# Block products accumulated in PSUM banks, and a third crossed pair in the MLP's second matrix

## What is computed

```python
def sq_relu_mlp(y, w_up, w_down):
    u = y @ w_up
    return jnp.square(jax.nn.relu(u)) @ w_down

for i in range(DEPTH):
    y = rmsnorm(h, norm_gains[i, 0])
    ...
    h = h + y
    h = h + sq_relu_mlp(rmsnorm(h, norm_gains[i, 1]), mlp_w_up[i], mlp_w_down[i])
```

## Time and profile before

| what | value |
|---|---|
| time of the kernel, median of 3 runs | 1192.2 us (1191.93 to 1194.11) |
| profiled execution, first to last instruction | 1190.5 us |
| PE busy | 1177.8 us, 99% of the span, 8809 matmuls |
| DVE busy | 1012.5 us, 85% |
| ACT busy | 696.4 us, 58% |
| POOL busy | 114.4 us, 10% |
| mean granted TensorE clock | 0.997 |
| HBM traffic | 110 GB/s |

### The profile page before, as it was taken

The page is one execution under the profiler, slowest core; times in us unless marked ns, Lnnn a source line. Parts: engine busy times, 40 slices in busy tenths (PEclk is TensorE's granted clock), DMA queues, the critical chain, the costliest instruction groups (busy, mean ns, idle before and its releaser), DMA issues.

```text
span 1190.5 us, 22996 instructions
## 1 busy us (share of the span) xinstructions
PE 1177.8 (99%) x8809; PEld 1126.1 (95%) x8809; DVE 1012.5 (85%) x1623; ACT 696.4 (58%) x1201; POOL 114.4 (10%) x171
## 2 busy tenths in 40 slices
PE   9999999999999999999999999999999999999998
PEld 8999999999999999999999999987899988989988
DVE  6889888888889989998568988887898998999973
ACT  6777877745534544535357887876545355445453
POOL 3221110100110110101010000000001001001000
PEclk9999999999999999999999999999999999999999
DMA  7343342433463563673231212223336535546532
GB/s 179 95 113 85 89 109 77 146 110 106 109 143 106 116 136 107 148 208 111 57 104 54 68 57 78 80 69 119 100 132 126 132 118 113 124 124 143 162 106 72
DMA packets 152376, 131.89 MB, mean 111 GB/s; under 512 B 23208, under 2 KB 143072, under 8 KB 152288
## 3 DMA queue, kind: packets, MB, share of 16 engines
q1 hardware_dynamic: 141600, 104.93, 29.9%
q0 software_dynamic: 10560, 25.66, 10.9%
q10 hardware_dynamic: 128, 0.09, 0.0%
HBM read 111.43 MB, written 19.24 MB: 110 GB/s over the span
## 4 chain that ended last, share of the span: by engine, by line
PE 64%; issue 22%; DVE 8%; ACT 3%; DMA 1%; POOL 1%; SPq 0%; DVEq 0%; POOLq 0%; ACTq 0%
PE ps L2335 24%; PE ps L2027 18%; PE ps L2262 15%; PE ps L2553 2%; PE ps L2082 1%; DVE lo L1611 1%; ACT hi L741 1%; PE ps L2100 1%; DVE u L1662 1%; DVE tbuf L1662 1%; DVE lof L1604 1%; DMA h_sum<-abuf 1%; DVE tbuf L1667 1%; DVE lo L1618 1%; ACT ah L1029 1%
## 5 line engine op out<-in xcount | busy, mean ns | idle before, releaser
L741 ACT ACTIVATE hi<-lof 128x1024 fp32r<-128x1024 f32 x80 | 82.8, 1052 | 136.6 <-DVE lof L1604 136.6
L2027 PE MATMUL ps<-yh,wh 128*128 128x264 f32 (+1 forms) x704 | 160.5, 302 | 0.0
L2027 PE MATMUL ps<-yh,wl 128*128 128x264 f32 (+1 forms) x704 | 155.3, 295 | 0.0
L2027 PE MATMUL ps<-yl,wh 128*128 128x264 f32 (+1 forms) x704 | 155.3, 294 | 0.0
L2335 PE MATMUL ps<-th,hi 128*128 128x264 f32 (+1 forms) x448 | 127.0, 283 | 0.5 <-DVE tbuf L1662 0.5
L2335 PE MATMUL ps<-tl,hi 128*128 128x264 f32 (+1 forms) x448 | 126.4, 282 | 0.0
L2335 PE MATMUL ps<-th,lo 128*128 128x264 f32 (+1 forms) x448 | 126.3, 282 | 0.0
L2262 PE MATMUL ps<-ah,hi 128*128 128x264 f32 (+1 forms) x448 | 116.3, 318 | 0.3
L1611 DVE TENSOR_TENSOR lo<-lof,hi 128x1024 fp32r<-128x1024 f32 x80 | 97.1, 1222 | 22.1 <-ACT hi L741 20.5
L2262 PE MATMUL ps<-al,hi 128*128 128x264 f32 (+1 forms) x448 | 115.6, 316 | 0.0
L2262 PE MATMUL ps<-ah,lo 128*128 128x264 f32 (+1 forms) x448 | 115.4, 316 | 0.0
(11 more groups left out here) (332 smaller groups left out, 3370.6 us busy)
## 6 DMA issues: line engine op xcount, KB each, us to landing
raw<-in_mlp_w_up_dram SPq DMA_DIRECT2D x32, 1024.0 KB, 5.6
raw<-in_mlp_w_down_dram SPq DMA_DIRECT2D x32, 1024.0 KB, 5.0
raw<-in_diff_w_in_dram SPq DMA_DIRECT2D x24, 512.0 KB, 3.7
raw<-in_mlstm_w_in_dram SPq DMA_DIRECT2D x16, 512.0 KB, 5.3
h_sum<-abuf POOLq DMA_DIRECT2D x24, 264.0 KB, 4.8
h_sum<-abuf POOLq DMA_DIRECT2D x24, 256.0 KB, 5.2
h_sum<-h POOLq DMA_DIRECT2D x16, 264.0 KB, 2.4
h<-h_sum POOLq DMA_DIRECT2D x2, 2112.0 KB, 10.2
```

Source lines behind the costliest of these rows:

```text
L741: return nc.scalar.activation(o, i, ACT.Copy, scale=scale)
L2027: last = mm(ps[:, bank + s, 0:w_], w[:, slot, kb, :], m[:, kb, t0:t0 + w_], start=(kb == 0 and n == 0), stop=(kb == CB - 1 and n == 2))
```

## The change

Down pair 5 of the first three groups becomes crossed too (`DOWN = 5`), which makes 23 crossed pairs a layer, and one plain down pair (4) is left ahead of them. The crossed pair's products are taken in the order A11, S1, A12, S2, S4, S3, A22 in three banks instead of seven: S2, S3 and A22 are accumulated on A11 in one bank, S4 on S1 in a second, and A12 has the third. Two sets of three banks (from bank 2 and from bank 5) alternate between crossed pairs. ACT copies the state of the first bank after A11 (`t1`) and after S2 (`u2`), and that of the second after S1 (`y1`); DVE makes three sums (C11 = t1 + A12, C12 = u2 + S4, C22 = y1 + S3), and C21 is what the first bank holds after A22: for an up pair DVE applies relu on it from PSUM (`relu_c21`), for a down pair ACT copies it out (`c21_out`). A product that continues a bank waits for the copy of what was in it (S2 for t1, S4 for y1, S3 for u2, A22 for C22), and A22 of a pair is done inside the next pair, after its S2 (or, before a plain pair, after six inner blocks of its first unit). The forms of the activations are used, and made ready, in the order S1, S2, S3, A22. The core of the diff:

```diff
+DOWN = 5
...
 def crossed_down(i):
 
-    return 0 <= i < PAIRS - 8 and i % 8 >= 6
+    return 0 <= i < PAIRS - 8 and i % 8 >= DOWN
...
-PRODUCTS = ("A11", "A12", "S2", "S3", "S1", "S4", "A22")
-
-
 def pe_order():
 
     for i in range(PAIRS):
-        yield from [(i, e) for e in (PRODUCTS if crossed(i) else (0, 1))]
+        if not crossed(i):
+            yield from [(i, 0), (i, 1)]
+            continue
+        yield from [(i, e) for e in ("A11", "S1", "A12", "S2")]
+        if crossed(i - 1):
+            yield i - 1, "A22"
+        yield from [(i, "S4"), (i, "S3")]
+        if not crossed(i + 1):
+            yield i, "A22"
...
-SUMS = {"C11": 1, "U2": 2, "U3": 3, "C22": 4, "U4": 5, "C12": 6, "C21": 7}
-FREED = {"A12": "C11", "S2": "U2", "S3": "U3", "S1": "U4", "S4": "C12", "A22": "C21"}
+N_DONE, N_READY, N_PLAIN, N_CROSSED, N_UPS, N_DOWNS, N_SENT = (len(x) for x in (DONE, READY, PLAINS, RANK, UPS, DOWNS, SENT))
+SUMS = {"C11": 1, "C12": 2, "C22": 3}
+BANK = {"A11": 0, "S2": 0, "S3": 0, "A22": 0, "S1": 1, "S4": 1, "A12": 2}
+SETS = (2, 5)
...
-                    wait(act, c_done, 7 * (ranks + RANK[i] - 1) - 7 + SUMS["U2"])
-                    copy(t1[:, 0:w], ps[:, bank_of(i, "A11"), 0:w]).then_inc(t1_done, 1)
+                def snap(i, name):
+
+                    to, made, sum_ = {"A11": (t1, t1_done, "C11"), "S1": (y1, y1_done, "C22"), "S2": (u2, u2_done, "C12")}[name]
+                    act.wait_ge(m_done, items + DONE[i, name])
+                    wait(act, c_done, len(SUMS) * (ranks + RANK[i] - 2) + SUMS[sum_])
+                    copy(to[:, 0:w], ps[:, bank_of(i, name), 0:w]).then_inc(made, 1)
+
+                def c21_out(i):
+
+                    act.wait_ge(m_done, items + DONE[i, "A22"])
+                    wait(act, h_sent[1], sent_before(layer, i))
+                    copy(ab[1][:, t0:mid], ps[:, bank_of(i, "A22"), 0:w]).then_inc(c21_down, 1)
...
+                    first_crossed = crossed_down(i) and i % 8 == DOWN
                     sent = sent_down(i - 1) and not crossed(i - 1)
                     if sent:
                         send(i - 1, 1)
-                    if first_crossed:
-                        block_hi(i, "S1")
-                        block_hi(i, "A22")
-                        snap(i)
                     if crossed(i + 1):
                         form_hi(i + 1, "S23")
-                    if crossed(i) and not first_crossed:
-                        snap(i)
+                    if crossed(i):
+                        snap(i, "A11")
+                    if crossed(i - 1) and is_up(i - 1):
+                        squares(i - 1, 0)
+                    if first_crossed:
+                        block_hi(i, "S3")
+                    if crossed(i):
+                        snap(i, "S1")
                     if crossed(i + 1):
                         form_hi(i + 1, "S14")
...
                     if crossed(i + 1):
                         natural_hi(i + 1, False)
                     elif 1 <= i < PAIRS - 1:
                         plain_hi(layer, i + 1, 1)
-                    if sent_down(i) and i % 8 == 5:
-                        block_hi(i, "S2")
-                        block_hi(i, "S3")
+                    if crossed(i):
+                        snap(i, "S2")
+                    if first_crossed:
+                        block_hi(i, "A22")
+                    if crossed(i - 1) and not crossed(i):
+                        squares(i - 1, 1)
...
-                    if crossed(i) and is_up(i):
-                        squares(i, 0)
+                    if sent_down(i) and i % 8 == DOWN - 1:
+                        block_hi(i, "S1")
+                        block_hi(i, "S2")
+                    if crossed(i - 1) and crossed(i):
+                        if is_up(i - 1):
+                            squares(i - 1, 1)
+                        else:
+                            c21_out(i - 1)
...
                     elif name == "C12":
                         dve.wait_ge(m_done, items + DONE[i, "S4"])
-                        dve.wait_ge(c_done, base + SUMS["U4"])
-                        o, x, y = to[0][:, second], u4[:, 0:w], p("S4")
+                        dve.wait_ge(u2_done, ranks + RANK[i])
+                        o, x, y = to[0][:, second], u2[:, 0:w], ps[:, bank_of(i, "S4"), 0:w]
                     else:
-                        dve.wait_ge(m_done, items + DONE[i, "A22"])
-                        dve.wait_ge(c_done, base + SUMS["U3"])
-                        o, x, y = to[1][:, first], u3[:, 0:w], p("A22")
+                        dve.wait_ge(m_done, items + DONE[i, "S3"])
+                        dve.wait_ge(y1_done, ranks + RANK[i])
+                        o, x, y = to[1][:, second], y1[:, 0:w], ps[:, bank_of(i, "S3"), 0:w]
                     V.tensor_tensor(o, x, y, ALU.add).then_inc(c_done, 1)
...
+                def relu_c21(i):
+
+                    dve.wait_ge(m_done, items + DONE[i, "A22"])
+                    V.scalar_tensor_tensor(tb[1][:, t0:mid], ps[:, bank_of(i, "A22"), 0:w], 0.0, rb[:, t0:mid],
+                                           ALU.max, ALU.mult).then_inc(c21_up, 1)
...
                     if crossed(i - 1):
-                        total(i - 1, "C21")
+                        total(i - 1, "C22")
                     elif i > 0 and not is_up(i - 1) and not in_tail(layer, i - 1) and not sent_down(i - 1):
                         evacuate(i - 1, 1)
-                    first_crossed = crossed_down(i) and i % 8 == 6
-                    if first_crossed:
-                        block_lo(i, "A22")
+                    first_crossed = crossed_down(i) and i % 8 == DOWN
                     if crossed(i + 1):
                         form_lo(i + 1, "S23")
                     if crossed(i - 1) and is_up(i - 1):
                         relu(i - 1, 1)
                         act_lo(i - 1, 0)
-                    if crossed(i):
-                        total(i, "C11")
+                    if first_crossed:
+                        block_lo(i, "S3")
                     if crossed(i + 1):
                         form_lo(i + 1, "S14")
                     if crossed(i):
-                        total(i, "U2")
-                    if is_up(i - 1):
+                        total(i, "C11")
+                    if is_up(i - 1) and not crossed(i - 1):
                         act_lo(i - 1, 1)
                     if crossed(i + 1):
                         natural_lo(i + 1, False)
                     elif 1 <= i < PAIRS - 1:
                         plain_lo(layer, i + 1, 1)
-                    if crossed(i):
-                        total(i, "U3")
+                    if first_crossed:
+                        block_lo(i, "A22")
+                    if crossed(i - 1) and is_up(i - 1) and not crossed(i):
+                        relu_c21(i - 1)
+                        act_lo(i - 1, 1)
...
                     if sent_down(i) and i % 8 == 4:
                         block_forms(i)
-                    elif sent_down(i) and i % 8 == 5:
+                    if sent_down(i) and i % 8 == DOWN - 1:
+                        block_lo(i, "S1")
                         block_lo(i, "S2")
-                        block_lo(i, "S3")
...
-                    if crossed(i):
-                        total(i, "C22")
-                        total(i, "U4")
-                    if sent_down(i) and i % 8 == 5:
-                        block_lo(i + 1, "S1")
+                    if crossed(i - 1) and is_up(i - 1) and crossed(i):
...
                     if crossed(i) and is_up(i):
                         relu(i, 0)
+                    if crossed(i - 1) and is_up(i - 1) and crossed(i):
+                        act_lo(i - 1, 1)
...
+                    if name == "A11" and before is not None:
+                        if crossed_down(before):
+                            pe.wait_ge(c21_down, N_DOWNS * layer + DOWNS[before])
                         else:
-                            pe.wait_ge(c_done, 7 * ranks + summed(last, FREED[product_]))
-                    elif down:
-
-                        if n == 0:
-                            pe.wait_ge(c_done, 7 * (ranks + RANK[i] - 1))
-                        elif n in (4, 6):
-                            pe.wait_ge(m_evac, plains + PLAINS[i - 1, n // 6])
-                    elif n < 7 and crossed(i - 1):
-
-                        pe.wait_ge(c_done, 7 * ranks + (summed(i - 1, FREED[PRODUCTS[n + 1]]) if n < 6 else summed(i - 2, "C21")))
+                            pe.wait_ge(c21_up, N_UPS * layer + UPS[before])
+                        if i % 8 == DOWN:
+                            pe.wait_ge(m_evac, plains + PLAINS[i - 1, 0])
+                    elif name == "S1" and before is not None:
+                        pe.wait_ge(c_done, sums + summed(before, "C12"))
+                    elif name == "A12" and before is not None:
+                        pe.wait_ge(c_done, sums + summed(before, "C11"))
```

(14 more changed lines are left out.)

117 lines of the change are left out of this document (50 added, 67 removed).

## The result

The kernel before took 1192.35 us (median of 4 runs on the same chip), the changed one **1280.13 us** (1277.7 to 1282.76): ratio 1.0735, 95% interval 1.0716 to 1.0753. The forecast was 1231.7, range 1205 to 1243. The sign was right, the size less than half: +39.5 was predicted and +87.8 measured, and the time lies outside the range.

A forecast was written before the change was run, and what follows sets the result against it. PE was taken to bound the kernel, nearly gapless inside an MLP. Terms -8.2 - 4.5 + 19.8 + 15.5 + 9.6 + 7.3 = +39.5 on 1190.5 gave 1230.0; the median, 1.7 above, 1231.7 us; range 1205 to 1243.

The forecast's parts named there:

- Part 1: Six plain pairs become crossed, which removes matmul time on PE: -8.2 us.
- Part 2: DVE's and ACT's load: waits fit in steady crossed pairs at no cost, and layer 1's DVE lateness is recovered: -4.5 us.
- Part 3: Activations' forms come too late for S1 of pair 13, 3.1 or 3.5 us in each of six groups: +19.8 us.
- Part 4: S2 of pair 13 waits for copy t1, behind the next pair's form on ACT, 2.6 us six times: +15.5 us.
- Part 5: Echo: the same copy is late again in pair 14, 1.5 or 1.7 us a group: +9.6 us.
- Part 6: Start of each MLP: S2 of pair 2 waits for the copy 2.0 or 2.5 us, plus half clock: +7.3 us.
- The DMAs: C22 of the next pair waits for a landed result DMA, just in time for A22: 0, bound +3 us.
- Only the forms are late: Rival: the copies in pairs 13 and 14 don't hold PE; +14.4 us, 1207 us; chance 0.08.
- gaps in the steady run: Sign that the prediction is wrong: PE gaps lying in the steady run; none were expected in pairs 8 to 11.
- the bank waits bite in every crossed pair: Rival: u2's copy comes late in steady runs, 0.3 us in about 35 further pairs; +10 us, 1242 us; chance 0.08.
- The clock loss is not absorbed: Rival: 1.4 us more after each of twelve longer gaps, at most half absorbed; +8 us, 1240 us; chance 0.12.
- rule on rotating banks: First rival's basis: S2, S4, S3 and A22 wait on their own bank in every pair; +10 us, chance 0.08.

The follow-up runs named there:

- e14: e13's orders with three crossed down pairs a group and the activations' four sums cut to 8 columns of each block: 1201.6 us.
- e13: Changed kernel with two crossed down pairs a group, the edits of e2, e3 and e4, and further reordering of ACT's copies and roundings and DVE's sums: 1192.29 us.
- e3: Changed kernel with C21's relu of the pair before placed ahead of pair i+2's weights' rest on DVE: 1263.4 us.
- e4: Changed kernel with a crossed down pair's second result sent in two DMAs, the next C22 waiting only for the first: 1255.6 us.
- e2: Changed kernel with ACT copying A11 (t1) ahead of rounding the next pair's S2 and S3 forms: 1270.4 us.
- e15: e13's orders with three crossed down pairs a group and the whole computation: 1222.8 us, ratio 1.0253.

## Why the prediction was right in sign and wrong in size

A wait costs PE more than its gap in the profile. The gap begins when the last matmul ends, 0.28 us after its start, where the next would have started after 0.12; and the product behind takes some 0.08 more. The prediction reckoned from start to start, so the second figure of a row, where it has two, is from start to start: how much longer than 1.455 us (layer 0) or 1.416 us (layer 1) the products in question took.

| step of the prediction | predicted | measured |
|---|---|---|
| Part 1, matmuls | -8.2 | not seen by itself. e14 less e13 is +9.3; longer crossed products make 12.1 of it and waits inside the plain pairs 3.1 or somewhat more, which leaves -6 to -7 (an estimate) |
| Part 2, DVE's lateness taken back | -4.5 | about -1 (e13, both MLPs) |
| Part 2, "I cost this part at nothing" | 0 | relu of C21: gaps 17.9, 24.8; 16.7 won by e3 |
| Part 3, forms | +19.8 | gaps 20.6, 21.6 |
| Part 4, t1 in pair 13 | +15.5 | 15.8 (gap and half clock together) |
| Part 5, t1 in pair 14 | +9.6 | gaps 7.5 (six of 1.13 to 1.32), 9.0 |
| Part 6, start of each MLP | +7.3 | gaps 1.94 and 2.32, with the slow products behind them 6.4 |
| The DMAs | 0, bound +3 | gaps 19.0, 26.5; 24.6 won by e4 |

**Part 3 held step by step.** Pair 11's C21 relu starts at 404.08, the fourth sum of the activations ends at 410.48 + 1.26, ACT rounds to 412.85 and `blocks_r` is done at 412.96 + 1.26 = 414.22; PE starts at 414.32. A11 of pair 13 started at 409.38, so S1 was wanted at 410.84 and is 3.5 us late for 3.1 predicted; in layer 1 it is 3.7 for 3.5. **Part 4 held as a sum:** 2.6 us a group from S1's start to S2's, over two products' time. In the group above 1.1 of it is the gap at 419.84, and most of the rest is S1 at half clock; in layer 0's first group S1 and A12 are both at half clock and S2 needs to wait no more. With it the rival "Only the forms are late" is out. Part 5 held too. Undoing the waits of Parts 4 to 6 in e2 gave 9.7 and not 31. A part of the reason is in e2's list, 6.8 us of waits for y1 and u2, which stand in the same queue, and S1's half clock stays where no wait hides it; the rest is not shown.

**The step that failed first is "The DMAs ... It just fits: 0, bound +3 in all".** The estimate put the copy of C21 at 9.6 us into the next pair, took 5.9 us past a landing from one row of layer 1, and set the 15.5 against a want at 15.6 to 16.0. But 15.5 is where the sum C22 starts. It lasts 0.42 us, and with that alone the step stood at 15.9 and was late in layer 1; with the 0.14 us that the trace has between its end and A22's start it is 16.1, late in both layers. In the trace pair 14 starts at 424.38 and the copy ends at 435.51, 11.1 in, later by 1.5 mostly because S2 waited (Part 5); that wait moves what A22 wants by as much, to 17.5 (441.89), and so costs nothing here. What does is the way past the landing: 442.50 - 435.51 = 7.0 us, not 5.9, and over the twelve passages 6.8 to 8.5. The sum is done at 18.5, and A22 is 1.2 us late. And it is not a single passage but a ring: where a second crossed down pair follows another, its 12.25 us come again, and the gap is 1.0 to 1.5 us at A22 of the group's second crossed down pair and 1.8 to 2.6 at A22 of its third. A margin of less than half a microsecond on a chain of 15 should have been a case of its own with a price, not a bound of 3. e4 measures the price: 24.6 us.

**The second is Part 2's "In the steady run of crossed pairs the waits fit. The tightest is S3's on the copy u2".** There I checked S3's wait on u2 and not A11's on C21's relu, which stands behind `natural_lo(i + 2, True)` on DVE, which is behind a rounding of ACT, which waits for PE. It has gaps of 10.0 us at up pairs, and of 7.9 at plain ones; e3 won 16.7. I had moved every instruction of ACT and DVE in my timetable for pairs 12 to 15 and none for pairs 8 to 12. The prediction named its own sign of this, gaps in the steady run, and that sign came. The rival nearest to it, "the bank waits bite in every crossed pair", named u2 and 10 us.

**The clock held in Parts 3 to 5.** There "I add nothing for the clock", since the waits behind take up the loss. The granted clock fell to 1.2 GHz at or within 1.5 us behind each of the six gaps of the forms, and Part 4's sum still came out at 2.6 us each time, whether S1, A12 or both were slow. Elsewhere the loss was paid: the clock also fell at three of the twelve waits for C22, some 4.5 us longer products that are part of the ring's 26.5, and at the start of layer 1's MLP, inside Part 6. Summed over the stretches that the trace marks with 1.2 GHz, PE worked 35.0 us at the lower clock in the changed kernel and none in e14, so at most 17.5 of the 19.5 us between their PE busy times (1196.3 and 1176.8, both with 8881 matmuls) are the clock's. The trace agrees in part with the Trainium skill's rule (TensorE: Matmul & The Clock Gate, HAM oscillation), that repeated gaps pay each time: the six of the forms did, of the other 45 waits in the MLPs only four did. The rival "The clock loss is not absorbed", about the longer gaps that the prediction foresaw, did not come true there.

Together, from start to start: Parts 3 to 6 are 52.8 us for 52.2 predicted, so these losses lay where I put them, and 51.3 (ring and relu) lay where I had put zero. With some 2 us in small pieces all crossed products of the MLPs are 106.0 us longer than their 1.455 or 1.416 us, against 7.4 in the kernel before. 106.0 - 7.4 - 8.2 of matmuls is 90.4, and the span grew by 89.4. That the prediction's four losses came out within 1 us in sum is partly luck: the forms were 1.8 above and Part 6 0.9 below.

The Trainium skill's rule on rotating banks (Perfetto Trace Analysis, Matmuls), taken as a rival, is not borne out as a price of each pair: in e13 every crossed pair still takes its seven products in three banks, and three such pairs take 30.68 us for 30.59 before.

**What stays open.** Why e13 is no faster than before: its MLP in layer 1 gained some 2.4 us over three groups and layer 0's lost 1.3, in small pieces. The wait of 1.99 us of the earlier trace rows and the half clock behind it are gone; in their place the products S4 and S3 of the first and last crossed pairs of a run take 0.1 to 0.6 us longer, and most of these pieces no wait in the trace names. What they are and whether they can be moved away wasn't tried. The third pair still costs 30.5 us in e15; that shorter sums on DVE would make it pay wasn't tried other than by leaving them out, and that did not make it pay (e14, 1201.6). No version was faster than the kernel before.
